# Attention probabilities transposed by a product with a diagonal of reciprocal sums

## The reference

```python
# B: 8 query heads, 2 key heads, blocks of 128 queries against 384 keys
s = einsum('bnqhgd,bnkhd->bnhgqk', qb, kw) * d ** -0.5     # masked to the band
m = maximum(max(s, -1), sink)
p = exp(s - m)
p = p / (sum(p, -1) + exp(sink - m))
o_b = einsum('bnhgqk,bnkhd->bnqhgd', p, vw) * silu(zb)
# C
s = einsum('bshd,bmhd->bhsm', q, k) * d ** -0.5
o_c = einsum('bhsm,bmhd->bshd', softmax(s), v) * silu(zc)
# all three groups
return h + concatenate([o_a, o_b, o_c]) @ w_out
```

## Time and profile before

| what | before |
|---|---|
| median of 3 runs | 2324.76 us (2321.35 to 2329.73) |
| the profiled execution | 2328.26 us |
| its span | 2326.6 us, mean granted TensorE clock 0.97 |
| TensorE busy over the span | 2164.2 us, 93% |
| VectorE | 1083.9 us, 47% |
| ScalarE | 660.8 us, 28% |
| GpSimd | 314.1 us, 13% |
| the attention stage | 1787.0 to 1953.6 us of the span |

### The profile page before, as it was taken

One profiled execution on the slowest core, in us unless ns is written; L12 is line 12 of the kernel. 1 busy time (PEld: TensorE's weight loads), 2 busy tenths in 40 slices (PEclk: granted clock), 3 DMA queues, 4 the chain that ended last, 5 costly groups with the idle time before them and its releaser, 6 DMA issues. The chain is left out here.

```text
span 2326.6 us, 28431 instructions
## 1 busy us (share of the span) xinstructions
PE 2164.2 (93%) x11264; PEld 1807.5 (78%) x11264; DVE 1083.9 (47%) x1854; ACT 660.8 (28%) x1004; POOL 314.1 (13%) x195
## 2 busy tenths in 40 slices
PE   6999999999999999999967999999987785999998
PEld 6888888888888888888856888888885454888887
DVE  7764444444444311221318666666644876323222
ACT  6511111111111110111115454444433665211110
POOL 4300000000000000000005444455401000000000
PEclk9999999999999999999988999999979997999999
DMA  6522122122122212212121221111111125534432
GB/s 225 191 85 81 55 81 81 54 81 81 55 81 81 81 58 78 81 54 81 46 84 55 81 93 58 64 64 64 46 64 55 55 82 184 214 127 149 158 126 90
DMA packets 78866, 210.87 MB, mean 91 GB/s; under 512 B 7328, under 2 KB 33056, under 8 KB 74560
## 3 DMA queue, kind: packets, MB, share of 16 engines
q1 hardware_dynamic: 69088, 174.04, 22.5%
q0 software_dynamic: 9696, 35.72, 3.9%
HBM read 165.11 MB, written 44.63 MB: 90 GB/s over the span
## 5 line engine op out<-in xcount | busy, mean ns | idle before, releaser
L73 PE MATMUL pr_acc<-x_hi,pr_w_lo 128*128 128x512 f32 (+1 forms) x1760 | 675.8, 384 | 26.4 <-DVE pr_w_lo L431 20.7
L74 PE MATMUL pr_acc<-x_lo,pr_w_hi 128*128 128x512 f32 (+1 forms) x1760 | 674.1, 383 | 0.0
L75 PE MATMUL pr_acc<-x_hi,pr_w_hi 128*128 128x512 f32 (+1 forms) x1760 | 674.0, 383 | 0.0
L73 PEld LDWEIGHTS pr_acc<-x_hi,pr_w_lo 128*128 128x128 f32 x1760 | 334.0, 190 | 91.9 <-issue 18.7
L74 PEld LDWEIGHTS pr_acc<-x_lo,pr_w_hi 128*128 128x128 f32 x1760 | 334.1, 190 | 63.8 <-issue 0.2
L75 PEld LDWEIGHTS pr_acc<-x_hi,pr_w_hi 128*128 128x128 f32 x1760 | 334.1, 190 | 63.4
L347 ACT ACTIVATE pr_w_hi<-pr_w_raw 128x1024 fp32r<-128x1024 f32 x118 | 124.9, 1060 | 749.3 <-PE pr_acc L75 728.4
L532 DVE TENSOR_TENSOR pr_padded<-pr_acc,pr_rstd 128x512 f32<-128x512 f32 x82 | 56.6, 692 | 518.4 <-PE pr_acc L75 518.3
L73 PE MATMUL ou_acc<-ou_w_hi,ou_m_lo 128*128 128x512 f32 x512 | 200.5, 392 | 18.1 <-DVE ou_w_lo L1842 18.1
L74 PE MATMUL ou_acc<-ou_w_lo,ou_m_hi 128*128 128x512 f32 x512 | 200.4, 391 | 0.0
L75 PE MATMUL ou_acc<-ou_w_hi,ou_m_hi 128*128 128x512 f32 x512 | 200.1, 391 | 0.0
(11 more groups left out here) (240 smaller groups left out, 2508.1 us busy)
## 6 DMA issues: line engine op xcount, KB each, us to landing
pr_w_raw<-in_w_in SPq DMA_DIRECT2D x118, 512.0 KB, 5.1
ou_w_raw<-in_w_out SPq DMA_DIRECT2D x32, 1024.0 KB, 4.9
proj_scratch<-pr_res POOLq DMA_DIRECT2D x50, 512.0 KB, 5.2
dl_qk<-proj_scratch SPq DMA_DIRECT2D x8, 1024.0 KB, 5.0
dl_grow<-gate_rows SPq DMA_DIRECT2D x8, 1024.0 KB, 7.6
ou_x_in<-in_x SPq DMA_DIRECT2D x8, 1024.0 KB, 7.1
out<-ou_res POOLq DMA_DIRECT2D x8, 1024.0 KB, 4.7
pr_res<-in_x_t SPq DMA_DIRECT2D x11, 512.0 KB, 5.9
```

Source lines behind the costliest of these rows:

```text
L73: pe.matmul(out, w_lo, x_hi, start=first, stop=False)
L74: pe.matmul(out, w_hi, x_lo, start=False, stop=False)
L75: return pe.matmul(out, w_hi, x_hi, start=False, stop=last)
```

## The change

VectorE stops after the reciprocals. GpSimd, which had nothing to do here, makes for every head a 128x128 matrix with the reciprocals of the 128 rows on its diagonal (identity times rsum, the new buffer diag of 2 x 4 matrices), and raises b_p with each. It waits for the reciprocals (b_d) and for the transposes that last read the same buffer (b_t). TensorE multiplies the unscaled probabilities, as the stationary operand, with that matrix, as the moving one, by an ordinary matmul in place of the transpose: the result in tp is transposed and scaled.

```diff
--- before.py
+++ after.py
@@ -1400,6 +1400,7 @@
         q_rope, q_tmp, q_mem = n.sb("q_rope", [P, 2, 4, P]), n.sb("q_tmp", [P, 4, P]), n.sb("q_mem", [P, 2, 4, P])
         sm = n.sb("sm", [P, 2, 2, W])
         prob = n.sb("prob", [P, 2, SEQ])
+        diag = n.sb("diag", [P, 2, 4, P])
         mx, negm, rsum, diff, sinks = (n.sb(x, [P, 2, 4]) for x in ("mx", "negm", "rsum", "diff", "sinks"))
         pt_b, pt_c = n.sb("pt_b", [P, 2, 3, 2, 4, P]), n.sb("pt_c", [P, 2, C_HEADS, P])
         out_b, out_c = n.sb("out_b", [P, 4, P]), n.sb("out_c", [P, 4, P])
@@ -1476,6 +1477,18 @@
         def _(pool):
             pool.memset(v_rows[:, 0], 0.0).then_inc(p_zero, 1)
             pool.memset(v_rows[:, BLK + 1], 0.0).then_inc(p_zero, 1)
+
+            def slot(h, parity, more, w):
+                for u in range(U):
+                    odd = (parity + u) % 2
+                    pool.wait_ge(b_d, h * 9 + (2 * u + 2 if u < LAST else 9))
+                    if not (h == 0 and u < 2):
+                        pool.wait_ge(b_t, h * 10 + (2 * u - 2))
+                    for i in range(2 if u < LAST else 4):
+                        pool.tensor_tensor(diag[:, odd, i], c["ident"][:], rsum[:, odd, i:i + 1].to_broadcast([P, P]),
+                                           ALU.mult).then_inc(b_p, 1)
+
+            blocks(slot)
 
         @block.scalar
         def _(act):
@@ -1587,17 +1600,9 @@
                     dve.tensor_tensor(rsum[:, odd, 0:2], rsum[:, odd, 0:2], sinks[:, odd, 0:2], ALU.add).then_inc(b_d, 1)
                     dve.wait_ge(b_d, h * 9 + (2 * u + 1))
                     dve.reciprocal(rsum[:, odd, 0:2], rsum[:, odd, 0:2]).then_inc(b_d, 1)
-                    dve.wait_ge(b_d, h * 9 + (2 * u + 2))
-                    for i in range(2):
-                        part = prob[:, odd, i * W:i * W + W]
-                        dve.tensor_scalar(part, part, rsum[:, odd, i:i + 1], None, ALU.mult).then_inc(b_p, 1)
                 else:
                     dve.wait_ge(b_e, h * 12 + 12)
                     dve.reciprocal(rsum[:, odd], rsum[:, odd]).then_inc(b_d, 1)
-                    dve.wait_ge(b_d, h * 9 + 9)
-                    for i in range(4):
-                        part = prob[:, odd, i * MEM_LEN:(i + 1) * MEM_LEN]
-                        dve.tensor_scalar(part, part, rsum[:, odd, i:i + 1], None, ALU.mult).then_inc(b_p, 1)
 
             def results(h, parity, which):
 
@@ -1687,12 +1692,13 @@
                         pe.wait_ge(b_td, h * 10 + (2 * u + i - 1))
                     if u < LAST:
                         for kc in range(3):
-                            last = pe.transpose(tp[:, i, bass.ts(kc, P)], prob[:, odd, i * W + kc * P:i * W + (kc + 1) * P],
-                                                c["ident"][:])
+                            last = pe.matmul(tp[:, i, bass.ts(kc, P)], prob[:, odd, i * W + kc * P:i * W + (kc + 1) * P],
+                                             diag[:, odd, i], start=True, stop=True)
                     else:
                         for head in range(C_HEADS):
                             at = head * MEM_LEN + i * P
-                            last = pe.transpose(tp[:, i, bass.ts(head, P)], prob[:, odd, at:at + P], c["ident"][:])
+                            last = pe.matmul(tp[:, i, bass.ts(head, P)], prob[:, odd, at:at + P], diag[:, odd, head],
+                                             start=True, stop=True)
                     last.then_inc(b_t, 1)
 
             def window_values(h):
```

## The result

| what | before | after |
|---|---|---|
| median of 4 runs | 2327.24 us (2321.35 to 2335.94) | 2355.75 us (2344.59 to 2359.82) |
| ratio | | 1.0102, 95% interval 1.0071 to 1.0132 |
| the profiled execution | 2328.26 us, span 2326.6 | 2344.59 us, span 2342.9 |
| VectorE busy | 1083.9 us | 1053.1 us |
| GpSimd busy | 314.1 us | 352.5 us |

The change costs 28.5 us between the medians and about 24 by the ratio, whose interval runs from 16.5 to 30.7 us; 27.0 was forecast. The whole times alone can't tell 27 from 20, so the steps have to be read from the traces. The two profiled executions differ by 16.3 only, while the attention alone is 26.0 longer in them (1967.23 - 1778.36 for 1950.13 - 1787.22). So the steps are compared inside the stage.

A forecast was written before the change was run, and what follows sets the result against it. No engine is full; the chain of waits inside an attention block bounds the stage. Six steady blocks at +3.59 us (+21.5), block 0 about +3.1 and block 7 +2.4 sum to +27.0, median 2351.8 us; range 2338 to 2366.

The forecast's parts named there:

- T1, T2 and T0, +0.70 each: TensorE's groups of six transposes after slots 1, 2 and 0: as products each adds 0.70 us to a steady block.
- T4, +0.94: TensorE's group of eight transposes after slot 4: as products it takes 0.94 us more a block.
- T2's start, +0.10: Wait before the group after slot 2: it starts 0.61 us after the reciprocals, for 0.51, now behind GpSimd's diagonal.
- T4's start, +0.72: Wait before the group after slot 4: four diagonals at 0.45 make it start 1.96 us after the reciprocals, for 1.24.
- T3 covered: Group of six after slot 3: its +0.70 us lies in the wait before T4 and adds nothing.
- -0.27 before T0: TensorE's wait for VectorE's scaling before the group after slot 0: it goes, 0.27 us less a block.
- The block: One steady block of 128 queries, between starts of the window values: terms sum to +3.59 us, +21.5 for six.
- The ends: Blocks outside the six steady ones: block 0 about +3.1 us, block 7 +2.4 us.
- Rival 1: Fuller TensorE work holds the clock up in the attention: 9.0 us come back, +18.0, 2343 us; chance 0.2.
- Rival 2: GpSimd's diagonals cost 0.80 us each, delaying T2 and T4: 5.34 a block, +40, 2365 us; chance 0.14.
- Rival 3: VectorE was the bound and a product costs no more than a transpose: not slower, down to 2314 us; chance 0.06.

The follow-up runs named there:

- e2: The kernel before, scaling on VectorE and no diagonals, with its 256 transposes made ordinary products with the identity; 2352.04 us.
- e1: The changed kernel with its GpSimd diagonals and waits, but transposing with the identity, the division by the sums left out; 2334.20 us.
- e4: The kernel before with transposes and no scaling at all, the division by the sums left out; 2301.05 us.
- after_again: The changed kernel run once more, in the same rounds as the kernel before; 2359.49 us, ratio 1.0116.
- v1_before: The kernel before with the next block's query rotation moved earlier on TensorE and VectorE's gating of window results moved to slot 2; 2316.01 us, ratio 0.993.
- v1_after: The changed kernel with the next block's query rotation moved earlier on TensorE and VectorE's gating of window results to slot 2; 2335.95 us, ratio 1.0009.
- v2: v1_before with the diagonal and products in slot 3 alone, VectorE scaling in the other slots; 2314.14 us, ratio 0.9936 to the kernel before.
- e3: The changed kernel with every diagonal made twice on GpSimd, once into a spare tile; 2372.14 us.

## Why the prediction was right, step by step

The forecast was 2352 and 2355.75 was measured, slower as forecast, 28.5 us for 27.0. The direction and the path are right; that the sum comes so near is in part luck, as the ends show. By its steps, for one block:

- **T1, T2 and T0, +0.70 each.** Right: 0.72 (1.44 for 0.72). e2 and e1 show from both sides that this is the price of a product in place of a transpose. The doubled records go with it; that they are two passes is the prediction's reading, and no run looks inside. The memory values in the trace of before had the price.
- **T4, +0.94.** 1.98 for 1.02, +0.96.
- **T2's start, +0.10.** +0.02: the diagonal took 0.405 for the 0.45 taken, and TensorE began 0.05 after it, not 0.07.
- **T4's start, +0.72.** +0.36, the one term of the block that was mis-sized, by half. Four diagonals in a row take 1.47 us, not 4 x 0.45 = 1.80. The mean of 405 ns was 0.045 below the figure taken, and the next diagonal begins before the last is through.
- **T3 covered.** Right: the wait before T4 is 0.91 (near 1.3 was forecast, with the later T4) and T3 has none.
- **-0.27 before T0.** Right, the wait is gone; T4's start to T0 is 2.83, of which T4 takes 1.98 and the scores 0.85.
- The block: +3.20 for +3.59.

The ends: from the first product of the stage to the first window values 34.5 us for 27.9, +6.6 where +3.1 was forecast. 2.3 of it stand ahead of T0, in products that the change leaves alone: from the first product to T0 it took 12.56 us for 10.28. e4 has 12.08 there, with no diagonals and no products in place of transposes, so this part is the clock of the execution and not the change. From T0 to the window values it was 21.9 for 17.6, +4.3. T0 and T2 hold TensorE 2.86 and 2.80 us, twice their normal time, but block 0 of the kernel before has a stretch at the low clock too, on T3, T4 and the scores (TensorE in order of time, kernel after):

```profile
1778.36 1.94 PE L1645 MATMUL at_ps<-c_ident,e_kvt 128*128 128x128 f32 x8 [9.27 <-PEq L585]
...
1790.92 2.93 PE L1695 MATMUL at_tp<-at_diag,at_prob 128*128 128x128 f32 x12 [1.31 <-POOL at_diag L1488]
1793.78 1.18 PE L1676 MATMUL at_ps<-e_k_pad,at_q_rope 64*128 64x384 f32 x4
...
1801.09 2.87 PE L1695 MATMUL at_tp<-at_diag,at_prob 128*128 128x128 f32 x12 [2.01 <-POOL at_diag L1488]
1803.89 1.25 PE L1676 MATMUL at_ps<-e_k_pad,at_q_rope 64*128 64x384 f32 x4
```

From the last steady block to the end it was 19.5 for 17.4, +2.1 for +2.4. In the middle, six blocks took 134.9 for 117.6: 6 x 3.20, less one stretch at the low clock (three for four) and less the 0.36 of the long wait in the kernel before. 6.6 + 17.3 + 2.1 = 26.0. So the sum was near by a term 0.36 too large in each block and one too small in block 0. The latter is luck for the greater part: 2.3 us of low clock ahead of T0 happened to make up for most of the other.

**Rival 1, the clock comes back: fell.** Products in place of transposes did not hold the clock up. With the wait of 2.0 before T2 the clock fell in 4 (before) and 5 (e1) of six blocks with transposes, and in 3, 4 and 4 (after, after_again, e2) with products; 9 of 12 and 11 of 18 are too few to tell whether the form counts at all. With waits of 1.65 or less it fell in no steady block: not behind T4's 1.65 in e1, and not at all in the 24 blocks of e4 (1.53 before T2), v1_before, v1_after and v2, transposes or products. So in the steady blocks every fall stands behind a wait of 1.98 or more. Not every such wait has one: the longest of the kernel before, 2.34, has none. And in block 0 the length of the last wait does not decide: T0 of the kernel after runs at the low clock behind a wait of 1.31, and that of v1_after behind one of 0.57. By the rule of the Trainium skill (TensorE: Matmul & The Clock Gate, Part 4) the full clock does not engage for transpose mode. These runs don't bear that out for transposes among products: e4 and v1_before have as many transposes as before and kept 1.00 through their steady blocks. What lies between 1.65 and 1.98, and what else decides, these runs do not show.

**Rival 2, GpSimd is dear: fell.** A diagonal took 0.405 us, not 0.80. e3, at twice the price, shows that it would have been slower indeed, 2372 us, through the clock as well.

**Rival 3, VectorE was the bound: fell.** e1 gave VectorE all of its relief and TensorE no growth, and the block stayed at 18.54. VectorE was the fullest engine, and most of its work lay beside TensorE's. The Trainium skill (TensorE: Matmul & The Clock Gate, Terms) calls transpose mode 4x faster for FP32; the pair measured here, 1.44 to 0.72, gives 2, and the prediction was right to go by its own pair.

## What to carry to other kernels

Count the records of an f32 transpose and of an f32 product before trading one for the other: here a 128x128 transpose holds TensorE 0.12 us and a product of the same shape 0.24, and what that costs depends on whether the group stands behind a wait. Work taken off the fullest engine is worth only what ends a wait, 1.8 of 4.1 us a block here even at no price, and what the clock gives back when the wait gets shorter, 1.1 more. The move gains in the one slot whose growth lies in another wait (v2_slot3), by 0.42 us a block, too little to tell in the whole time. Look first at why the engine waits: two steps put in another order gained 0.7%, where moving the scaling lost 1%.

## What the hardware showed that was not expected

A longer wait can cost more than its length. Lengthening T4's wait from 0.91 to 2.35 in e3 brought a stretch at 1.2 GHz behind it in every block, 1.6 us on top. In e4, where T2's wait fell from 1.98 to 1.53 and those before T4 and T0 went, there was none left in the steady blocks; which of the waits did it was not tried apart.

The other is the spread of this kernel, 2322 to 2339 us over 21 runs of before. The traces show one source of such differences in a stretch of the delta rule's work ahead of the attention, which no edit here touches. Busy time and clock of that stretch in the kernel before (first), in the changed kernel (second), and in the changed kernel once more, in after_again (third):

```profile
1714.00:1743.00 29.00, 27.49 (x133) 27.49 (x134) 6.48 (x16) 8.69 (x11) 0.00 (x0) 0.53 0.25 82
```

```profile
1714.00:1743.00 29.00, 26.63 (x212) 26.64 (x213) 9.75 (x24) 9.27 (x13) 0.41 (x1) 0.88 0.29 93
```

```profile
1714.00:1743.00 29.00, 24.01 (x113) 24.01 (x114) 6.47 (x16) 6.79 (x7) 2.34 (x1) 0.57 0.36 119
```

In the first TensorE stays near half clock while it is busy almost all the time (27.49 of 29.00), in the second it is at 0.88 and leaves 212 matmul records in place of 133. The third is the same code as the second and has 0.57, so it is not the edit. All ten profiles fall into these two sorts. Where the clock is 0.53 to 0.57 (before, e1, e2, v1_before, v1_after, after_again), the attention starts at 1787 to 1792 us; where it is 0.83 to 0.88 (after, e3, e4, v2), at 1778 to 1780. That is most of why the two profiled executions of the changed kernel lie 18 us apart, 16.3 and 34.2 above the one of before. What decides between the two was not tried and stays open.
